# A two-chunk weight ring loaded in halves, each half with its own semaphore

## The reference, cut to what matters

```
proj = rms_norm(x) @ w_in                       # 1024 x 6688
y_a  = (b * conv3(c * u)) @ w_out_a             # 512 -> 1024
y_b  = attention(q, kv, k_rope) @ w_out_b       # q_lat @ w_uq, kv_lat @ w_ukv before it
y_c  = silu(layer_norm(conv31(gv * sigmoid(gg)))) @ w_out_c
x   += (sigmoid(ga)*y_a + sigmoid(gb)*y_b + sigmoid(gc)*y_c) @ w_o
x   += experts(rms_norm(x))                     # 32 experts, 2 for each token, 3 MB of weights each
x   += sigmoid(rms_norm(x) @ w_ple_gate) * (p @ w_ple)
```

## Time and profile before

| | us |
|---|---|
| runs | 1302.49, 1296.05, 1296.95 |
| median | 1296.95 |
| profiled execution | 1295.48 |
| its span | 1293.7 |

### The profile page before, as it was taken

How to read it: one execution, slowest core, us unless ns; L and a number is a source line. 1 busy time by engine, 2 the same in 40 slices (tenths; PEclk the granted TensorE clock), 3 DMA queues, 4 the chain that set the end, 5 groups by cost and what they waited for, 6 DMA issues and landing times.

```text
span 1293.7 us, 21151 instructions
## 1 busy us (share of the span) xinstructions
PE 1136.4 (88%) x7828; PEld 892.3 (69%) x7828; DVE 564.4 (44%) x1125; ACT 371.1 (29%) x627; POOL 154.5 (12%) x174
## 2 busy tenths in 40 slices
PE   5998879998779998888899978899996999888897
PEld 5985879888655554446889767898984555444497
DVE  3579885335441111114646889643356111111254
ACT  4332333223312221114343124332232122111242
POOL 0022320001001000000102132200100110000001
PEclk7999999999889999999989989999997999999997
DMA  5433853554359999992525258254433999999722
GB/s 162 134 96 119 330 191 103 178 160 147 130 205 417 417 418 417 416 417 87 179 72 173 73 195 325 91 171 147 150 128 127 390 416 419 418 416 418 288 67 81
DMA packets 136280, 300.49 MB, mean 232 GB/s; under 512 B 12656, under 2 KB 101616, under 8 KB 119792
## 3 DMA queue, kind: packets, MB, share of 16 engines
q1 hardware_dynamic: 136176, 299.18, 62.4%
HBM read 298.11 MB, written 1.05 MB: 231 GB/s over the span
## 4 chain that ended last, share of the span: by engine, by line
PE 52%; DVE 14%; SPq 14%; DMA 11%; issue 5%; ACT 3%; POOL 1%; ACTq 0%; POOLq 0%; DVEq 0%
PE ps L659 49%; SPq L533 12%; DMA ring<-in_w_in_dram 5%; DVE work L1583 4%; DMA gu_ring<-in_w_exp_up_dram 3%; PE ps L662 3%; DVE wsplit L1488 3%; DMA ring<-in_w_exp_up_dram 2%; ACT wsplit L1076 2%; DVE work L1514 1%; DMA ring<-in_w_out_b_dram 0%; ACT work L1076 0%; DVE ps L1565 0%; DMA work<-in_positions_dram 0%; DVE wsplit L1845 0%
## 5 line engine op out<-in xcount | busy, mean ns | idle before, releaser
L659 PE MATMUL ps<-h_pair,wsplit 128*128 128x256 f32 x3264 | 421.7, 291 | 29.0 <-ACT wsplit L1076 23.0
L659 PEld LDWEIGHTS ps<-h_pair,wsplit 128*128 128x128 f32 x3264 | 409.6, 197 | 39.7 <-issue 36.9
L1488 DVE TENSOR_TENSOR wsplit<-ring,wsplit 128x1024 fp32r<-128x1024 f32 x136 | 171.0, 1262 | 166.5 <-ACT wsplit L1076 160.5
L1076 ACT ACTIVATE wsplit<-ring 128x1024 fp32r<-128x1024 f32 x136 | 139.2, 1053 | 230.4 <-DMA ring<-in_w_in_dram 145.8
L659 PE MATMUL ps<-gu_ring,hT 128*64 128x256 f32 x1280 | 158.3, 390 | 30.7 <-DMA gu_ring<-in_w_exp_up_dram 22.3
L659 PEld LDWEIGHTS ps<-gu_ring,hT 128*64 128x64 f32 x1280 | 91.5, 139 | 98.6 <-issue 37.1
L659 PE MATMUL ps<-work,ring 128*128 128x256 f32 (+2 forms) x640 | 143.0, 380 | 1.4 <-DMA ring<-in_w_out_b_dram 0.9
L1076 ACT ACTIVATE work<-ps 128x512 f32 (+5 forms) x124 | 68.4, 555 | 236.6 <-PE ps L662 167.1
L1811 DVE TENSOR_TENSOR pT<-pT,ps 128x128 f32<-128x128 f32 x64 | 18.4, 288 | 268.4 <-ACT pT L1238 268.4
L659 PEld LDWEIGHTS ps<-work,ring 128*128 128x128 f32 (+2 forms) x640 | 111.5, 177 | 28.8 <-issue 3.8
L1583 DVE SCALAR_TENSOR_TENSOR work<-work,convT 128x256 f32<-128x256 f32 x240 | 114.0, 542 | 0.2
(11 more groups left out here) (188 smaller groups left out, 961.9 us busy)
## 6 DMA issues: line engine op xcount, KB each, us to landing
ring<-in_w_in_dram SPq DMA_DIRECT2D x52, 1024.0 KB, 5.3
gu_ring<-in_w_exp_gate_dram SPq DMA_DIRECT2D x40, 1024.0 KB, 21.6
gu_ring<-in_w_exp_up_dram SPq DMA_DIRECT2D x40, 1024.0 KB, 21.9
down_ring<-in_w_exp_down_dram SPq DMA_DIRECT2D x40, 1024.0 KB, 22.0
lent_down<-in_w_exp_down_dram SPq DMA_DIRECT2D x24, 1024.0 KB, 22.1
ring<-in_w_exp_gate_dram SPq DMA_DIRECT2D x12, 1024.0 KB, 20.3
ring<-in_w_exp_up_dram SPq DMA_DIRECT2D x12, 1024.0 KB, 21.2
lent_gate_up<-in_w_exp_gate_dram SPq DMA_DIRECT2D x12, 1024.0 KB, 21.1
```

The costliest lines, as they stand in the source:

```text
L659: return nc.tensor.matmul(o, lhsT, rhs, start=first, stop=last)
L1076: return nc.scalar.activation(o, i, ACT.Copy)
L1488: TT(tile_split[:, m, 1, :, :], tile_of(name, m), tile_split[:, m, 0, :, :].bitcast(F32), ALU.subtract).then_inc(tile_low, 1)
```

## The change

Each chunk is loaded as two halves, each with a wait of its own for the bytes it overwrites, and a semaphore of its own. For a split product a half is one tile of 128 columns, and the ring now holds tile 0's 1024 numbers per partition first and tile 1's behind them (runs of 512 B in memory). For yab the halves are the two transfers that there were. For the others (ukv, uq, yc, pp) a half is the first or second half of the blocks of 128 rows. ACT waits for half m before tile m; ya waits for half 0 and yb for half 1; everything else waits for both. Where the overwritten chunk is a split product, half 0 waits for its low tile 0 and half 1 for its low tile 1; where it is yab, half 0 waits for ya and half 1 for yb; otherwise both wait for its last unit.

```diff
-        chunk_loaded = [sem(f"chunk_loaded{i}") for i in range(RING)]
+        chunk_loaded = [[sem(f"chunk_loaded{i}_{half}") for half in range(2)] for i in range(RING)]
...
-        def wait_chunk(eng, l, name):
-
-            n = CI[name]
-            slot = n % RING
-            upto = sum(2 if c[:3] == "yab" else 1 for c in CHUNKS[slot:n + 1:RING])
-            whole = sum(2 if c[:3] == "yab" else 1 for c in CHUNKS[slot::RING])
-            eng.wait_ge(chunk_loaded[slot], l * (16 * whole) + 16 * upto)
+        def wait_chunk(eng, l, name, halves=(0, 1)):
+
+            slot, n = CI[name] % RING, CI[name] // RING + 1
+            for half in halves:
+                eng.wait_ge(chunk_loaded[slot][half], l * (16 * NC // RING) + 16 * n)
...
-            return ring[:, CI[name] % RING, :].rearrange("p (k n) -> p k n", k=DC)[:, :, m * P:(m + 1) * P]
+            return ring[:, CI[name] % RING, m * DC * P:(m + 1) * DC * P].rearrange("p (k n) -> p k n", k=DC)
...
-                if before in SI:
-                    sp.wait_ge(tile_low, NTILES * of_layer + 2 * SI[before] + 2)
-                else:
-                    sp.wait_ge(unit_ready, NU * of_layer + LAST_UNIT[before] + 1)
-                sp.sem_inc(wait_carried, 1)
+                parts = source(l, name)
+                if name in SI:
+                    parts = [parts[0][:, :, 0:P], parts[0][:, :, P:2 * P]]
+                elif len(parts) == 1:
+                    k = parts[0].shape[1] // 2
+                    parts = [parts[0][:, 0:k, :], parts[0][:, k:2 * k, :]]
                 at = 0
-                parts = source(l, name)
-                for i, src in enumerate(parts):
+                for half, src in enumerate(parts):
+                    if before in SI:
+                        sp.wait_ge(tile_low, NTILES * of_layer + 2 * SI[before] + half + 1)
+                    elif before[:3] == "yab":
+                        sp.wait_ge(unit_ready, NU * of_layer + UI["y" + "ab"[half] + before[3:]] + 1)
+                    else:
+                        sp.wait_ge(unit_ready, NU * of_layer + LAST_UNIT[before] + 1)
+                    sp.sem_inc(wait_carried, 1)
...
-                    sp.dma_start(dst, src).then_inc(chunk_loaded[n % RING], 16)
+                    sp.dma_start(dst, src).then_inc(chunk_loaded[n % RING][half], 16)
...
-                    wait_chunk(pe, l, chunk_of(name))
+                    wait_chunk(pe, l, chunk_of(name), {"ya": (0,), "yb": (1,)}.get(name[:2], (0, 1)))
...
-                wait_chunk(act, l, name)
                 for m in range(2):
+                    wait_chunk(act, l, name, (m,))
```

## The result

The changed kernel takes 1285.12 us (median of 6 runs, 1282.56 to 1288.52) against 1297.59 us for the kernel before (6 runs, 1296.05 to 1302.49): ratio 0.9896, 95% interval 0.9875 to 0.9917, 12.5 us less. The profiled execution took 1284.47 us, its span is 1282.7 us. So the profiled span is 11.0 us shorter and the medians are 12.5 us apart.

The account below looks back on a forecast made before the run. PE was taken as nearly the bound in the gates, late loads as the rest (experts DMA-bound, convolution DVE-bound). 10.7 + 0.45 + 2.3 = 13.4 us, taken as 13, gave 1284 us; own range 1280 to 1289, with rivals 1279 to 1293.

Parts of the forecast that it names:

- the terms 10.7 and 0.45: Gates: 10.7 us of load waits gone over six periods in two layers, and 0.45 us ahead of yc0 in layer 0.
- earlier release and earlier use: Gates: half 0 issued 2.0 us (3.4 at gc) earlier; ACT starts at half 0's landing, 1.3 us before the whole's.
- Lands at least 1.3 us earlier: At gg0, half 0 lands this much before the whole did; part of the 2.3 us gain over two layers.
- half 0 is issued at the same moment as the whole today: At gg0, first load behind SP's small loads: issue time unchanged; part of the 2.3 us gain.
- it passes on: gg0's 2.3 us gain reaches further, since DVE's taps and PE's chain to the queries start from these products.
- 34 ns: Split chunks' loads: assumed DMA engine time per 512 B run, 4.4 us a MB in place of 3.3.
- Rivals B: A 512 B run costs what a 1024 B run does; gg0's gain gone, b1 5 us late: 1296 us, chance 0.07.
- C: Short strided runs cost more than counted at c1, u1, b1; slower from 53 ns, 1306 us at 64 ns; chance 0.05.
- The cover of 4.9 us: Convolution stretch: b1 landed by 170.2 us, copied at 175.15; three chunks' dearer runs take 3.3 us of it, costing nothing.
- rivals A: Gates: another link (DVE's low tile, ACT's sigmoid) holds PE in half the places; gain 6 us, 1291 us, chance 0.08.
- D: Half 0 isn't issued earlier because SP stands at an earlier wait; about 5 us gained, 1292 us, chance 0.04.
- The 2 us a load: Fixed DMA cost from the Trainium skill; if paid serially, three chunks take 6 us of cover and gain is 11 us.

Follow-up runs that it names:

- Experiments 2 to 4: Changed kernel with the early release undone, the earlier use undone, and both undone: 1286.80, 1294.64 and 1310.28 us.
- late release: Changed kernel, but both halves wait for the last use of the chunk they overwrite; half waits kept: 1286.80 us, ratio 0.9902 to the kernel before.
- one wait: Changed kernel, but ACT waits for both halves before tile 0, and ya and yb for both; early release kept: 1294.64 us, ratio 0.9966.
- experiment 6: Changed kernel, but ya and yb both wait for both halves: 1290.29 us, ratio 0.9928 to the kernel before.
- experiments 6, 7 and 8: experiment 6, experiment 7, and the changed kernel with ACT copying c0's high tiles before the first two softmax rows, the last 1284.77 us, ratio 0.9889.
- gates only, experiment 5: Changed kernel with half waits and early release kept only for the twelve gate chunks: 1294.03 us, ratio 0.9953 to the kernel before.
- neither, experiment 4: Changed kernel with early release and earlier use both undone, still two transfers with 512 B runs: 1310.28 us, ratio 1.0089 to the kernel before.
- experiment 7: Changed kernel with each half tile of the split chunks loaded as two transfers with 256 B runs: 1284.91 us, ratio 0.9893 to the kernel before.
- the changed kernel again: Changed kernel run once more without any edit: 1286.27 us, ratio 0.9901 to the kernel before.

## Why the prediction was right

**The size.** 1284.0 was forecast, 1285.12 measured: 12.5 us less against 13. The range and the side were right.

**The gates.** The period without waits was put at 27.84 us from four rows of layer 1; it is 27.64. From ga0 to wo0 layer 0 went from 122.49 to 115.78 us and layer 1 from 121.42 to 115.78 us: 12.35 us in both, where the terms 10.7 and 0.45 make 11.15. Of the 1.2 us more, 0.8 us lie in the six periods (11.5 us gained against 10.7: six times 0.2 us, less 0.4 us because the boundary at wo0 costs 0.9 us a layer and not 0.7), and 0.4 us between ga0 and ga1 (0.69 and 0.15 us gained against 0.45 in one layer).

**What of the edit pays.** The prediction named earlier release and earlier use side by side and added their leads (4.7 us at gc). Experiments 2 to 4 show that in the gates the second makes the first unnecessary: late release costs nothing that can be measured. The condition that it gave, that the lead be larger than the 1.06 us of idle, was met there by early use alone, with 1.3 us (a landing after 4.0 us in place of 5.3).

**ya.** Forecast as one wait of 0.95 us that goes. It went, but its worth is larger than the row before showed: once gc is in time, PE reaches ya sooner. With one wait it is 1.26 us at its first place in layer 0, and 1.17 and 1.20 us in layer 1; alone (experiment 6) it costs 2.65 us in the profile, and some 4 us by ratios whose intervals overlap. A wait that another wait hid doesn't show in the trace before.

**gg0: right in size, wrong in its steps.** 2.3 us were forecast from its idle, and the idle is gone. Both steps given for it failed. "Lands at least 1.3 us earlier" after its issue was wrong: behind the small loads half 0 lands 7.4 us after its issue, and the whole before landed after 7.3 (in layer 1 7.2 and 7.5).

```profile
L529 SPq DMA_DIRECT2D ring<-in_w_in_dram x1: 1243/1243/1243, 49.4 to 49.4; - x1
DMA to landing us min/median/max: 7.3/7.3/7.3
```

```profile
L534 SPq DMA_DIRECT2D ring<-in_w_in_dram x1: 384/384/384, 47.4 to 47.4; - x1
DMA to landing us min/median/max: 7.4/7.4/7.4
```

And "half 0 is issued at the same moment as the whole today" was wrong: SP issues it at 47.42 us, where the whole went at 49.36, and this is what ends the idle. q2's half 0, released early, goes 2.2 us before its whole did (39.36 against 41.52), and SP's eight issues of small loads behind it, from 41.98 in both, are over sooner; the longest takes 1.05 us in place of 2.05. Why they are shorter wasn't tried. SP's queue after, from q2 on:

```profile
39.36 2.50 SPq L534 DMA_DIRECT2D ring<-in_w_in_dram  x2
...
47.42 7.41 SPq L534 DMA_DIRECT2D ring<-in_w_in_dram  x4
```

With late release the same issue was at 49.14, and the idle was back in layer 0 (0.94 us; in layer 1 half 0 landed after 5.4 us and there was none). gg0 starts 1.8 us sooner than in the earlier trace rows (no bracket at 56.17):

```profile
56.17 6.11 PE L664 MATMUL ps<-h_pair,wsplit 128*128 128x256 f32 x48
62.12 2.87 PE L664 MATMUL ps<-ones,work 128*128 128x1 f32 x24
64.85 5.34 PE L664 MATMUL ps<-h_pair,wsplit 128*128 128x256 f32 x31
```

But gv0 then takes 7.2 us, from 64.85 to the next product's broadcast at 72.06, where it took 5.83. The windows say why (columns as in the earlier trace rows, the clock third from the end): at 65.5 to 67.5 us the granted clock is 0.50, the 1.2 GHz level, with no idle of PE in it or in the 8 us before it, and 11 matmuls in 2 us; at 69 to 71 us it is 1.00, the 2.4 GHz level, with 19.

```profile
65.50:67.50 2.00, 2.00 (x11) 2.00 (x11) 0.45 (x2) 0.00 (x0) 1.44 (x2) 0.50 0.85 204
69.00:71.00 2.00, 2.00 (x19) 2.00 (x19) 1.23 (x1) 0.62 (x1) 0.00 (x0) 1.00 0.00 0
```

From gg0's start to ukv this makes 27.94 us where the kernel before took 26.31, so 1.6 us of the 1.8 are taken back. It is not a step that the prediction had. Its "it passes on" holds: in all ten profiles ga0 of layer 0 starts 105.6 to 106.8 us behind ukv, and where the stretch took 26.3 us without idle ahead of it (experiments 6, 7 and 8) ga0 starts at 188.01, 188.74 and 187.92, 1.1 to 1.9 us before the 189.87 of the kernel before. The profile's own gain is 11.0 us for the same kind of reason: at wo0 of layer 1 the changed kernel is 13.15 us ahead, and then the rest of w_o takes it 10.91 us (934.67 to 945.58, clock 0.50 from 935 to 938) where the kernel before took 9.41, both behind 1.94 us of idle.

In ten profiles, two layers each, the stretch from gg0's start to ukv took 26.3 or 26.4 us eight times, 27.8 to 27.9 us eight times, and 29.3 us four times, so steps of 1.5 us. Of the eleven with no idle ahead of gg0, six took 26.3 or 26.4 us, four 27.8 to 27.9, one 29.4 us. Of the nine with 0.9 us of idle or more two took 26.3, four 27.8, and three 29.3. The three are the two of "gates only" (idle 2.54 and 2.68 us) and layer 1 of "neither" (2.92 us), and they are all the cases with more than 2 us of idle. That a longer stop of PE here is followed by a lower clock is what these rows suggest; it wasn't tried by itself. It would explain why experiment 5 lost more than the 5.2 us of its idle, of which 2.3 us stood there before the change.

**The shorter runs.** 34 ns was taken, 30 ns came out, between the ends of 26 and 51.5. Rivals B and C, which needed 51.5 and 53 ns, are refuted; with 256 B the chunk costs 2.2 us more by the share than before, and even that didn't show. The cover of 4.9 us was read too large: b1 was issued at 161.04 and landed 10.2 us later, at 171.2, so 3.9 us before its copy (175.15). With it and three chunks the edge is at 36 ns a run, and at 38 ns with the prediction's own 4.9 us, not at the 44 ns that it named. That 3 x 2.2 = 6.6 us didn't make b1 late with 256 B has two reasons in the traces. From c1's first issue to b1's landing it takes 27.4 us in the kernel before (from 143.84), 29.3 in the changed one (from 142.01) and 32.0 with 256 B (from 140.98), so the price in the queue is 1.9 and 4.6 us for the three chunks. And the early release puts c1's issue 1.8 us sooner. So 3.7 us of cover are left in the changed kernel, and 1.0 us with 256 B: its price was nearly all that the stretch can hide. That the edit's first effect is a loss (experiment 4) was not in the prediction: it priced the runs only in the stretch with the expert loads, and not ahead of gc, where the whole load's landing sets PE's start. With half tiles the price is still there, but falls where PE has other work.

**The rivals A and D** are refuted by the gate periods. The 2 us a load, paid one after the other, that the prediction held against itself would have put b1's landing 18 us later in experiment 7, which has four loads a chunk for one; the three chunks took 4.6 us longer.

## What to carry to other kernels

When a wait for a load stands ahead of work that begins with a part of it, price a semaphore for that part and a sooner release of the space, but don't add the two, since they can cover the same wait. In the gates here the semaphore was enough alone; at gg0, where the part landed no sooner after its issue, it took the release too. A wait's worth can be read from start-to-start intervals of groups that had no wait elsewhere in the same trace, better than from the idle in front of each. And look for waits hidden behind the one that you remove, and for what the same edit costs before its benefit, by running it with the benefit taken out.

## What was not expected of the hardware

PE's granted clock falls to the 1.2 GHz level also where PE shows no idle in the 8 us before, and the fall differs between executions of one kernel: the profile after has it from 65 to 68 us and the changed kernel again from 65 to 71 us, while "late release" and the kernel before have none in layer 0. From gg0 to ukv the first costs PE 1.6 us and the second, twice as long, 3.1 us. Two profiles of the changed kernel were 10 us apart (spans 1282.7 and 1292.7 us), of which ga0's start shows 2.1 us by the first 190 us.

Strided loads of 512 and of 256 B runs cost the DMA engines 18% and 67% more time than 1024 B runs for the same bytes (3.9 and 5.5 against 3.3 us a MB, by the share), not two and four times as much. And half a load needn't land sooner after its issue than the whole: 4.0 against 5.3 us at gc1, but 7.4 against 7.3 us at gg0, behind the small loads.
